# Mixer A's softmax rows left undivided, the inverse sums applied to the outputs after their trip through memory

## The reference, cut to what matters

```
for each of 3 (window, dilation) patterns:
    p   = exp(s - m);  den = sum(p);  o = (p @ v) / den;  lse = m + log(den)
alpha = softmax(lse over the 3 patterns);  o_A = sum(alpha * o)
mixed = sigmoid(gate_a) * (o_A @ w_up_a) + sigmoid(gate_b) * (o_B @ w_up_b)
```

## Time and profile before

| | |
|---|---|
| time, median of 3 runs | 1992.44 us |
| span of the profiled execution, first to last instruction | 1985.4 us |
| what lies around the span, if the execution took the median | 7.0 us |
| TensorE busy | 1845.1 us (93%) |
| VectorE busy | 1165.0 us (59%) |
| ScalarE busy | 564.1 us (28%) |
| GpSimd busy | 537.7 us (27%) |
| granted TensorE clock, mean | 0.970 |

### The profile page before, as it was taken

How to read it: one execution, slowest core, us unless ns; L and a number is a source line. 1 busy time by engine, 2 the same in 40 slices (tenths; PEclk the granted TensorE clock), 3 DMA queues, 4 the chain that set the end, 5 groups by cost and what they waited for, 6 DMA issues and landing times.

```text
span 1985.4 us, 24743 instructions
## 1 busy us (share of the span) xinstructions
PE 1845.1 (93%) x8514; PEld 1480.5 (75%) x8514; DVE 1165.0 (59%) x1812; ACT 564.1 (28%) x958; POOL 537.7 (27%) x296
## 2 busy tenths in 40 slices
PE   5799898998899999978999889999999999999996
PEld 5577776776677777766887767888888888888884
DVE  8447984799579967996644556333333333333336
ACT  4224641464236524664321333100000000000002
POOL 5321121202211221102332112333333333333335
PEclk9899998999999999998999989999999999999997
DMA  5311111011101111126322001111111111111112
GB/s 215 100 45 39 37 44 47 29 48 51 52 27 48 40 52 38 35 85 225 137 74 85 32 15 50 43 51 44 53 42 53 42 53 42 53 42 53 42 42 85
DMA packets 43239, 118.71 MB, mean 60 GB/s; under 512 B 6160, under 2 KB 14608, under 8 KB 43024
## 3 DMA queue, kind: packets, MB, share of 16 engines
q1 hardware_dynamic: 21312, 75.66, 11.4%
q10 hardware_dynamic: 21840, 41.96, 6.3%
HBM read 97.67 MB, written 18.87 MB: 59 GB/s over the span
## 4 chain that ended last, share of the span: by engine, by line
PE 68%; DVE 19%; issue 7%; ACT 3%; ACTq 1%; DMA 1%; DVEq 0%; POOL 0%; SPq 0%; POOLq 0%
PE ps L358 60%; DVE r_row L1257 4%; PE ps L470 4%; DVE pt L1239 2%; DVE r_row L1255 2%; PE ps L499 2%; DVE raw L1148 1%; DVE rows L1224 1%; PE ps L484 1%; DVE o_low L1231 1%; ACTq L797 1%; DVE rms L1115 1%; DVE h L1465 1%; DVE raw L1164 1%; DVE rows L1258 1%
## 5 line engine op out<-in xcount | busy, mean ns | idle before, releaser
L324 POOL TENSOR_SCALAR w_hi<-w_stage 128x1024 fp32r<-128x1024 f32 x138 | 152.5, 1105 | 1414.3 <-issue 709.5
L358 PE MATMUL ps<-n_hi,w_hi 128*128 128x512 f32 x1536 | 402.4, 403 | 26.8 <-DVE raw L1148 16.3
L358 PE MATMUL ps<-n_hi,w_lo 128*128 128x512 f32 x1536 | 391.5, 396 | 0.0
L358 PE MATMUL ps<-n_lo,w_hi 128*128 128x512 f32 x1536 | 390.5, 395 | 0.0
L326 POOL TENSOR_TENSOR w_lo<-w_stage,w_hi 128x1024 fp32r<-128x1024 f32 x138 | 364.1, 2639 | 11.5
L358 PEld LDWEIGHTS ps<-n_hi,w_hi 128*128 128x128 f32 x1536 | 291.5, 193 | 96.5 <-DVE raw L1148 21.7
L358 PEld LDWEIGHTS ps<-n_lo,w_hi 128*128 128x128 f32 x1536 | 288.2, 190 | 60.1
L358 PEld LDWEIGHTS ps<-n_hi,w_lo 128*128 128x128 f32 x1536 | 287.5, 190 | 58.7
L1325 DVE TENSOR_TENSOR h<-ps,h 128x512 f32<-128x512 f32 (+1 forms) x192 | 132.0, 690 | 157.0 <-PE ps L358 156.6
L1014 ACT ACTIVATE a_hi<-u_f 128x1024 fp32r<-128x1024 f32 x22 | 23.4, 1062 | 475.4 <-DVE u_f L1431 475.4
L1423 DVE TENSOR_TENSOR u_f<-ps,rms 128x512 f32<-128x512 f32 x44 | 30.4, 691 | 205.3 <-PE ps L358 205.3
(11 more groups left out here) (165 smaller groups left out, 2212.0 us busy)
## 6 DMA issues: line engine op xcount, KB each, us to landing
w_stage<-weights_in SPq DMA_DIRECT2D x138, 512.0 KB, 3.3
gates_scratch<-raw ACTq DMA_DIRECT2D x16, 512.0 KB, 2.9
o_scratch<-o_sum ACTq DMA_DIRECT2D x128, 32.0 KB, 1.8
n_lo<-o_scratch ACTq DMA_DIRECT2D x8, 512.0 KB, 5.5
g_a<-gates_scratch ACTq DMA_DIRECT2D x8, 512.0 KB, 3.6
g_b<-gates_scratch ACTq DMA_DIRECT2D x8, 512.0 KB, 4.8
h<-x_t_in ACTq DMA_DIRECT2D x8, 512.0 KB, 8.7
out_t<-h ACTq DMA_DIRECT2D x16, 256.0 KB, 2.1
```

What stands on the lines that cost most here:

```text
L324: pool.tensor_scalar(w_hi[:, b, :], stage[:, b, :], 1.0, 1.0, ALU.mult, ALU.mult).then_inc(w_rounded, 1)
L358: ins = pe.matmul(bank, w[:, b, c:c + P], mv(k), start=(first and n == 0), stop=(last and n == total - 1))
```

## The change

ScalarE's exp writes each row sum into its own column of a new tile `den` (128 x 2 heads x 8 blocks). VectorE no longer takes a reciprocal and multiplies for each unit of A. It takes one reciprocal of all 16 columns in slot 16, ScalarE stores them in slot 17 to `rden_scratch`, one head at a time, and TensorE's transposes of A's rows wait for the exp instead. In `LAST`, ahead of the load of each tile of A, ScalarE issues two loads that spread one head's 1024 inverse sums over 64 partitions each, into tiles that are free by then. VectorE multiplies each loaded tile of A by them (`normal_o`) before ScalarE makes its hi part.

```diff
+        rden_d = nc.dram_tensor("rden_scratch", [2 * PAIRS, T], F32, kind="Internal").ap()
...
+        rden_bc = (sin_t, cos_t, swap, bias_A)
...
                     if u < 16:
-                        pe.wait_ge(pA_ready, i * 16 + (u + 1))
+                        pe.wait_ge(exp_ready, i * 16 + (u + 1))
...
                             act.activation(row, row, ACT.Exp, scale=HD ** -0.5, bias=stat[:, 1, c:c + 1],
-                                           accum_out=stat[:, 2, c:c + 1]).then_inc(exp_ready, 1)
+                                           accum_out=den[:, ORDER[u][0], ORDER[u][1]:ORDER[u][1] + 1]
+                                           ).then_inc(exp_ready, 1)
...
+                    if s == 17:
+                        store_rden(i)
+                    if s == 27:
+                        act.wait_ge(rden_out, i * 32 + 32)
                     u = s - LAG - 3
                     if 0 <= u < UNITS:
                         store_o(i, u)
...
                         for k in LOAD_O[s]:
+                            if k < PAIRS:
+                                for h in range(2):
+                                    act.dma_start(rden_bc[k][h * HD:(h + 1) * HD, :],
+                                                  rden_d[2 * k + h].partition_broadcast(HD)).then_inc(rden_in[k], 16)
                             act.dma_start(n_lo[:, k, :].bitcast(F32), o_d[k]).then_inc(tile_in[k], 16)
...
             def round_o(k):
-                act.wait_ge(tile_in[k], 32)
+                if k < PAIRS:
+                    act.wait_ge(o_normal, k + 1)
+                else:
+                    act.wait_ge(tile_in[k], 32)
                 act.activation(n_hi[:, k, :], n_lo[:, k, :].bitcast(F32), ACT.Copy).then_inc(o_hi_s, 1)
+
+            def store_rden(i):
+                act.wait_ge(rden_ready, i + 1)
+                for h in range(2):
+                    act.dma_start(rden_d[bass.ds(i * 2 + h, 1), :].rearrange("o (b p) -> p (o b)", p=P), den[:, h, :],
+                                  allow_slow_non_contiguous=True).then_inc(rden_out, 16)
...
+            def normal_o(k):
+
+                dve.wait_ge(tile_in[k], 32)
+                dve.wait_ge(rden_in[k], 32)
+                part = n_lo[:, k, :]
+                dve.tensor_tensor(part, part.bitcast(F32), rden_bc[k][:], ALU.mult).then_inc(o_normal, 1)
...
                     u = s - 1
-                    if 0 <= u < 16:
-                        width = (ORDER[u][1] + 1) * P
-                        c = u % 4
-                        dve.wait_ge(exp_ready, i * 16 + (u + 1))
-                        link(dve.reciprocal(stat[:, 3, c:c + 1], stat[:, 2, c:c + 1]))
-                        row = rows[:, u % 4, 0:width]
-                        dve.tensor_scalar(row, row, stat[:, 3, c:c + 1], None, ALU.mult).then_inc(pA_ready, 1)
+                    if u == 15:
+                        dve.wait_ge(exp_ready, i * 16 + 16)
+                        dve.reciprocal(den[:], den[:]).then_inc(rden_ready, 1)
...
+                    if plan is LAST and s in ROUND_O:
+                        normal_o(ROUND_O[s])
                     if plan is LAST and s - 1 in ROUND_O:
                         o_rest(ROUND_O[s - 1])
```

More of the change, by code:

```diff
@@ L160, in build @@
         stat = keep("stat", [P, 4, 4], F32)
+        den = keep("den", [P, 2, NB], F32)
         def phase(*tensors):
@@ L234, in build @@
         logits_full, logits_free = sem("logits_full"), sem("logits_free")
-        max_ready, exp_ready, pA_ready, pB_ready = sem("max_ready"), sem("exp_ready"), sem("pA_ready"), sem("pB_ready")
+        max_ready, exp_ready, pB_ready = sem("max_ready"), sem("exp_ready"), sem("pB_ready")
+        rden_ready, rden_out, rden_in = sem("rden_ready"), sem("rden_out"), [sem(f"rden{k}_in") for k in range(PAIRS)]
+        o_normal = sem("o_normal")
         abs_ready, soft_ready, arg_ready = sem("abs_ready"), sem("soft_ready"), sem("arg_ready")
@@ L1280, in round_ @@
                 assert local[0] == links
-            LINKS = UNITS + 16 + 3 * 16 + 4
+            LINKS = UNITS + 3 * 16 + 4
             dve.wait_ge(bias_in, 32)
```

## The result

| | before | after |
|---|---|---|
| median of the runs on one chip, taken in turn | 1992.28 us (4 runs, 1989.3 to 1993.64) | 2003.61 us (4 runs, 2002.12 to 2005.03) |
| ratio after / before | | 1.0067, 95% interval 1.0048 to 1.0086 |
| span of the profiled execution | 1985.4 us | 2000.2 us |
| granted TensorE clock, mean | 0.970 | 0.964 |

The ratio is a loss of 13.3 us (9.6 to 17.1), the medians differ by 11.3 us, the two profiled spans by 14.8 us. The forecast was 2001.7 us with a range of 1997 to 2010.

What follows compares the result with a forecast made beforehand. It took A's half to run at TensorE's pace and B's at VectorE's. Terms 0 + 0 + 0 + 9.3 us on the 1985.4 us span, with 7.0 us around it, gave 2001.7 us, range 1997 to 2010.

Steps and rivals of the forecast that it cites:

- the end of round 4: Where outputs return from memory: eight more DMA issues and four multiplies, last output store 9.3 us later.
- Removed work in A's half: 57.9 us of VectorE work removed where TensorE sets the pace: worth 0.
- Rival (a): Relief carries into B's half: 13.4 us gained less 9.3 lost, 1988.3 us, faster; chance 0.07.
- The handover: Where A hands over to B: VectorE waits for unit 17's copy anyway, so B starts at the same time; 0.
- The scattered stores: Two stores of `den` on ScalarE's queue in slot 17 each round, in 4-byte pieces: taken as 0.
- Rival (d): Scattered stores hold ScalarE or the queue 2 to 7 us a round: 2010 to 2030 us; chance 0.09.
- the ring: End of round 4: multiply, hi part, next partial sum and two adds follow each other without slack, 3.2 us a tile.
- The loads' bandwidth: End of round 4: 8 x 256 KB more to transfer, landed before needed; taken as 0, bounds 0 to 5 us.
- rival (c): Spreading loads or queue are the bound: 3 to 5 us on top, up to 8; 2005 to 2010 us; chance 0.13.
- Rival (b): End of round 4 half hidden in waits: 1993 to 1997 us, no change; chance 0.11.
- The term for GpSimd's work beside VectorE's: Which VectorE operations of B meet GpSimd's work may change: 1.5 us each way, for the range.
- The 7.0 us around the span: Time outside the profiled span, added to the forecast span of 1994.7 us to give 2001.7 us.

Runs made afterwards that it cites:

- nodiv_hoist: Kernel before without its 64 reciprocals and multiplies (A's outputs undivided), `soft_ready` wait moved ahead of the instruction before the scan: 1987.95 us, ratio 0.9984.
- early_hoist_nomul: Changed kernel with spreading loads in slots 20 to 27, `soft_ready` wait moved ahead, four multiplies removed (A's outputs undivided): 1991.98 us, ratio 1.0000.
- before_twice: Kernel before with VectorE's row multiply done a second time for units 0 to 13 of A, 56 more multiplies: 1989.0 us, ratio 1.0003.
- after_nomul: Changed kernel without its four multiplies at the end, A's outputs undivided, spreading loads kept in place: 2004.22 us, ratio 1.0085.

## Why the prediction was right, and where it was off

The mechanism that it named carries most of the loss. The time lay 1.9 us above the forecast, and the loss by the ratio 4.0 us above the 9.3 that were forecast: a term of about that size was missing, and the range had not been made wide for it. That the time still fell in the range, and the direction with it, rests on the end of round 4, which was right to 0.8 us. By its steps:

- **Removed work in A's half, 0.** Right to within some 3 us. 57.9 us less (`nodiv_hoist`) brought 3.2 us (1.4 to 5.0), of which 0.9 lie at the handover in its trace; for the other 2.3 no trace shows a cause, and `early_hoist_nomul`, with the same work gone, is at 1.0000. 36 us more (`before_twice`) cost 2.1 us in the trace and none that the times tell. TensorE stayed at 76.00 of 76 us. Rival (a) needed 13.4 us and fell.
- **The handover, 0.** Nearly. VectorE stands waiting for the copies of units 16 and 17, 3.76 us instead of 1.04, but unit 16 did start straight behind VectorE's own work before, with no wait ahead of it, so it gained a little: 0.25 us a round at unit 17, 0.75 us in all. The step that erred was to take TensorE as the pace up to there for every unit.
- **The scattered stores, 0.** Right. Two issues took 1.03 us, in the forecast 1.0 to 1.5. The packets under 512 B rose from 6160 to 14608, 8448 more, of which 4 x 2 x 1024 = 8192 are the 4-byte pieces. The Trainium skill, "DMA: Bandwidth & Descriptors", "Rules for kernel authors", has one descriptor for each element of such a dimension, and the trace agrees on that. The pieces of a round moved in 1.3 us, far under both of the forecast's bounds from above, 12 and 80 us, and `early_hoist_nomul` has all these stores and a ratio of 1.0000. Rival (d) fell.
- **The end of round 4, 9.3 us.** Measured 10.1. Its two parts: the ring, 4.9 us, with multiplies 3.35, 3.26 and 3.14 us apart where the forecast had 3.2; and the issues. These were mis-sized. I took 0.48 us for each of eight loads, and got a slot 33 that is "some 4 us late". In the trace the issues of slot 30 take 3.66 us (891.58 to 895.24) instead of the 1.08 of the earlier trace rows, 2.6 us for four, so 0.65 us each; those of slot 31 take 3.54 us (897.50 to 901.04) instead of 0.93, again 2.6, and the eight make 5.2 us. In the earlier trace rows there was 1.08 / 2 = 0.54 us for a load, which I passed over for the store's 0.48. The second wait of TensorE moved with it, as forecast: 0.64 us at 927.02, 0.68 before. One sign failed: TensorE's wait was to be 9 us longer than 5.50 and is 4.1 us longer. The forecast had its start late by nearly the right amount, but left its own last products where they were, and these come 6.0 us later.
- **The loads' bandwidth, 0.** Right in the sum and narrow in its reason. The first multiply waited for no DMA, but the loads of the outputs took 8.1 us to landing instead of 5.5, and without the multiplies the outputs' stores came up to 1.79 us late. The 0 held only because the ring covered it: `after_nomul` shows that the queue's own end stands 1.2 to 2.1 us below, and so rival (c) was nearer than its reasons against made it. Rival (b) fell with the ring, which had no slack.
- **The term for GpSimd's work beside VectorE's, in the range: nothing.** L1255 on 896 columns takes 1.21 us on the mean before and 1.21 after (L1282).
- **The 7.0 us around the span.** They are 2, and 5 us of a quick execution. The sum came to no harm, since it was compared with the median from which the 7.0 had been worked out.
- **The term that was missing: 3.9 us of idle time.** "From there on nothing differs", and B's halves at the same length: both false. B's scan waits for a register instruction that the change has left behind, in 45 units at 0.09 us. The order of the two programs was there to be read with its waits before the forecast; I had read only which operations went away, and not what their waits had prepared for others. With it, and the end and the handover as measured, the sum is 10.1 + 3.9 - 0.75 = 13.2 us; the ratio makes 13.3 us (9.6 to 17.1). So close a fit is luck: the interval is 7.5 us wide, and the 3.9 us cost less than that by the traces.

## What to carry to other kernels

Before work is taken off an engine, find the half of the loop that runs at that engine's pace; 58 us taken from the other half brought 3 us here, while four operations of 1.2 us and eight DMA issues at a seam where the next stage waits cost 10. Count a DMA issue as work of the engine that issues it, by the row of its own kind, and put loads that are known early where that engine has room. When waits are removed, compare the register instructions of the two programs: a value that one wait computed may be what a later one lived on.

## What the runs showed of the hardware that I had not expected

- A register instruction between two dependent VectorE operations lengthened the gap between them from 0.03 to 0.12 us on the mean, 45 times, where it waited for the first of them; placed ahead of it, it cost nothing (idle before the scans 2.2 us in each kernel that has it so).
- Two stores of 1024 pieces of 4 bytes are issued in 1.03 us, as fast as two plain loads of 512 KB (1.08 us), and their 2048 pieces moved in 1.3 us.
- Issuing a load that spreads one row over 64 partitions took 0.47 to 0.62 us, and each plain load between such loads 0.60 us (once 1.49, in `after_nomul`), against 0.54 for the first two and 0.47 for the next two before.
- A 32 KB store, which lands in 1.8 us on the median, took 5.8 to 8.9 us behind the loads of the fourth round's end (`after_nomul`), so that its buffer was still waited for four units later, 1.79 and 0.88 us.
